# Two more quad products in the 512-column form, and a ScalarE copy ahead of a high part

## The reference

```python
D_FF = 2816
def swiglu(h, w_gate_up, w_down):
    gate, up = jnp.split(h @ w_gate_up, 2, axis=-1)
    return (jax.nn.silu(gate) * up) @ w_down
...
    h = h + swiglu(rms_norm(h, ffn_norm[layer]), ffn_w_gate_up[layer], ffn_w_down[layer])
```

## Time and profile before

| | before |
|---|---|
| median of 3 runs | 1299.03 us (1298.75 to 1299.54) |
| the profiled execution's own time | 1299.24 us |
| its span, first to last instruction | 1297.4 us |
| granted PE clock | 1.000, the upper level (2.4 GHz) |
| PE busy | 1285.9 us (99%), 7292 matmuls |
| DVE busy | 917.2 us (71%) |
| ACT busy | 556.1 us (43%) |

### The profile page before, as it was taken

One profiled execution on the slowest core, in us unless ns is written; L12 is line 12 of the kernel. 1 busy time (PEld: TensorE's weight loads), 2 busy tenths in 40 slices (PEclk: granted clock), 3 DMA queues, 4 the chain that ended last, 5 costly groups with the idle time before them and its releaser, 6 DMA issues.

```text
span 1297.4 us, 19358 instructions
## 1 busy us (share of the span) xinstructions
PE 1285.9 (99%) x7292; PEld 1102.0 (85%) x7292; DVE 917.2 (71%) x1413; ACT 556.1 (43%) x1162; POOL 255.7 (20%) x290
## 2 busy tenths in 40 slices
PE   9999999999999999999999999999999999999998
PEld 8888778888888998899988878888888998899986
DVE  7988857356689984388945778556789983488842
ACT  6347455124533660056622347425423650166612
POOL 0222144212322002100021136413221012000020
PEclk9999999999999999999999999999999999999999
DMA  7334322232333323333323331133333423333232
GB/s 248 102 94 113 93 78 84 82 97 89 123 98 98 114 82 101 97 114 110 99 85 113 109 115 56 51 97 97 98 97 98 122 90 98 100 112 99 82 98 98
DMA packets 96844, 130.69 MB, mean 101 GB/s; under 512 B 5329, under 2 KB 62161, under 8 KB 96753
## 3 DMA queue, kind: packets, MB, share of 16 engines
q1 hardware_dynamic: 94976, 127.29, 31.8%
q10 hardware_dynamic: 1776, 2.18, 0.6%
HBM read 124.67 MB, written 2.10 MB: 98 GB/s over the span
## 4 chain that ended last, share of the span: by engine, by line
PE 90%; DVE 5%; issue 2%; ACT 2%; DMA 0%; SPq 0%; DVEq 0%; ACTq 0%
PE ps L807 18%; PE ps L811 18%; PE ps L810 18%; PE ps L986 4%; PE ps L988 4%; PE ps L987 4%; PE ps L975 3%; PE ps L976 1%; PE ps L1469 1%; PE ps L1468 1%; PE ps L1465 1%; DVE ff_u L2180 1%; PE ps L1298 1%; PE ps L1314 1%; PE ps L1327 1%
## 5 line engine op out<-in xcount | busy, mean ns | idle before, releaser
L729 POOL TENSOR_SCALAR w_hi<-raw 128x1024 fp32r<-128x1024 f32 x156 | 182.7, 1172 | 941.0 <-PE ps L988 366.8
L1497 DVE TENSOR_TENSOR w_lo<-raw,w_hi 128x1024 fp32r<-128x1024 f32 x161 | 201.2, 1253 | 182.1 <-POOL w_hi L729 178.6
L807 PE MATMUL ps<-f_hi,w_hi 128*128 128x512 f32 x720 | 281.2, 391 | 0.2 <-DVEq L1893 0.2
L811 PE MATMUL ps<-f_hi,w_lo 128*128 128x512 f32 x720 | 280.2, 389 | 0.0
L810 PE MATMUL ps<-f_lo,w_hi 128*128 128x512 f32 x720 | 280.2, 389 | 0.0
L986 PE MATMUL ps<-z_both,quad_hi 128*128 128x256 f32 x640 | 182.2, 285 | 4.5 <-ACT copied L2744 4.5
L987 PE MATMUL ps<-z_both,quad_hi 128*128 128x256 f32 x640 | 181.1, 283 | 0.0
L807 PEld LDWEIGHTS ps<-f_hi,w_hi 128*128 128x128 f32 x720 | 135.1, 188 | 28.8 <-DVEq L1893 0.4
L811 PEld LDWEIGHTS ps<-f_hi,w_lo 128*128 128x128 f32 x720 | 135.1, 188 | 28.4
L810 PEld LDWEIGHTS ps<-f_lo,w_hi 128*128 128x128 f32 x720 | 135.2, 188 | 27.8
L986 PEld LDWEIGHTS ps<-z_both,quad_hi 128*128 128x128 f32 x640 | 121.5, 190 | 9.8 <-ACT copied L2744 6.9
(11 more groups left out here) (276 smaller groups left out, 2276.1 us busy)
## 6 DMA issues: line engine op xcount, KB each, us to landing
quad_raw<-in_w_gate_up SPq DMA_DIRECT2D x64, 512.0 KB
raw<-in_w_down SPq DMA_DIRECT2D x44, 512.0 KB
raw<-in_w_gate_up SPq DMA_DIRECT2D x48, 256.0 KB
raw<-in_w_out SPq DMA_DIRECT2D x20, 512.0 KB
raw<-in_w_in SPq DMA_DIRECT2D x19, 512.0 KB
raw<-in_xa_wkv SPq DMA_DIRECT2D x16, 512.0 KB
raw<-in_w_in SPq DMA_DIRECT2D x17, 256.0 KB
raw<-in_xa_wq SPq DMA_DIRECT2D x8, 512.0 KB
```

The lines of the kernel that those rows point to most:

```text
L729: pool.tensor_scalar(w_hi[:, slot], raw[:, slot], 1.0, 1.0, ALU.mult, ALU.mult).then_inc(s_hi, 1)
L807: ins = pe.matmul(o, whi, rhi, start=start, stop=False)
L811: return pe.matmul(o, wlo, rhi, start=False, stop=stop)
L1497: dve.tensor_tensor(w_lo[:, slot], raw[:, slot], w_hi[:, slot].bitcast(F32), ALU.subtract).then_inc(s_lo, 1)
```

## The change

Products 3 and 7 take the `quad_product_apart` form too, so four of the seven have it. The low and high data of such a product lie in neighbouring rows of one tile (`zq_r`) instead of far apart in `z_both`. Banks 2 and 3 of a quad now hold a low-data half as well: `copy_third_sum` copies a whole bank (512 columns, was 256), and DVE gets a new instruction per quad, `second_tile_apart`, which adds these halves to the second output tile. The silu, the multiply and the release of banks that waited for `second_tile` now wait for it. On ACT, `f_high(n - 1, 0)` moves from ahead of two weight high parts and `copy_second_sum` to just behind that copy.

```diff
@@ PE
-                        quad_product(l, q, 3, d, False)
+                        quad_product_apart(l, q, 3, d_wide, d)
                         pe.wait_ge(s_cp, COPIED[q, "u2"])
-                        quad_product(l, q, 7, a, False)
+                        quad_product_apart(l, q, 7, a_wide, a)
@@ DVE
+                    def second_tile_apart(n):
+
+                        ff = ff_u if n % 2 else ff_g
+                        dve.wait_ge(s_c, 3 * (QUAD0[l, c] + n) + 1)
+                        dve.tensor_tensor(halves(ff[:, 1, :]), halves(ff[:, 1, :]), bank_pair(qg, n, 2, 1),
+                                          ALU.add).then_inc(s_c, 1)
+
                     def gated(n, p):
 
                         q = QUAD0[l, c] + n
-                        dve.wait_ge(s_c, 2 * q + 2 - p)
+                        dve.wait_ge(s_c, 3 * q + 3 - p)
...
                         second_tile(n)
+                        second_tile_apart(n)
@@ ACT
-                        act.activation(home(qg, n, 3), home(qg, n, 1), ACT.Copy).then_inc(s_cp, 1)
+                        act.activation(ps[:, bank(qg + n, 3), :], ps[:, bank(qg + n, 1), :], ACT.Copy).then_inc(s_cp, 1)
...
                         weight_high(c, n, 4)
-                        if n and not up:
-                            f_high(n - 1, 0)
                         if more:
                             weight_high(c, n + 1, 5)
                             weight_high(c, n + 1, 2)
                         copy_second_sum(n)
+                        if n and not up:
+                            f_high(n - 1, 0)
...
                         copy_third_sum(n)
                         if not up:
-                            act.wait_ge(s_c, 2 * q + 1)
+                            act.wait_ge(s_c, 3 * q + 2)
                             act.activation(ff_g[:, 1, :], ff_g[:, 1, :], ACT.Silu).then_inc(s_q_silu, 1)
```

More of the change, by code:

```diff
@@ L70 @@
 Z_HIGHS = (1, 2, 4, 5, 6, 7, 3)
+APART = (2, 4, 3, 7)
+Z_STEP = {slot: 2 if slot in [Z_SLOT[i] for i in APART] else 1 for slot in range(8)}
+Z_UNIT = {slot: 4 * sum(Z_STEP[before] for before in range(slot)) for slot in range(8)}
+Z_HIGH_UNIT = {i: 4 * sum(Z_STEP.values()) + 4 * j for j, i in enumerate(i for i in Z_SLOT if i not in APART)}
 Z_LOWS = (1, 5, 2, 6, 3, 7, 4)
@@ L269, in trunk @@
         zf_hi, zf_lo = f_hi[:, 4:12, :], f_lo[:, 4:12, :]
[L270 to L274, removed]
+        zq = at("zq", [P, 60, QHALF], F32, z_zh)
+        zq_r = at("zq_r", [P, 60, QHALF], F32R, z_zh)
         quad_raw = at("quad_raw", [P, SLOTS, 4, 2 * P], F32, z_raw)
@@ L344, in low_and_high, with z_rows @@
         def low_and_high(i, k):
-            lo, hi = 4 * Z_SLOT[i] + k, 32 + 4 * (i - 1) + k
-            return z_both[:, lo:hi + 1:hi - lo, :]
+            u = Z_UNIT[Z_SLOT[i]] + 2 * k
+            return zq_r[:, u:u + 2, :]
+        def z_rows(i):
+            step = 2 if i in APART else 1
+            lo = Z_UNIT[Z_SLOT[i]]
+            hi = lo + 1 if i in APART else Z_HIGH_UNIT[i]
+            return slice(lo, lo + 3 * step + 1, step), slice(hi, hi + 3 * step + 1, step)
         def halves(tile):
@@ L975, in quad_product_apart @@
                     pe.matmul(both, kind_hi(i)[:, k, :], low_and_high(i, k), start=False, stop=False, skip_group_check=True)
-                    ins = pe.matmul(o, kind_lo(q, i)[:, k, :], zq_hi[:, i - 1, k, :], start=False, stop=k == 3,
+                    ins = pe.matmul(o, kind_lo(q, i)[:, k, :], low_and_high(i, k)[:, 1, :], start=False, stop=k == 3,
                                     skip_group_check=True)
@@ L984, in quad_product @@
                     whi, wlo = kind_hi(i)[:, k, :], kind_lo(q, i)[:, k, :]
-                    zh, zl = zq_hi[:, i - 1, k, :], zq_lo[:, Z_SLOT[i], k, :]
+                    lo, hi = z_rows(i)
+                    zh, zl = zq_r[:, hi, :][:, k, :], zq_r[:, lo, :][:, k, :]
                     pe.matmul(o, whi, zh, start=start and k == 0, stop=False, skip_group_check=True)
@@ L1003, in quads @@
                     b, a, d = home(g0, n, 0), home(g0, n, 1), home(g0, n, 2)
-                    b_wide, a_wide = ps[:, bank(g0 + n, 0), :], ps[:, bank(g0 + n, 1), :]
+                    b_wide, a_wide, d_wide = (ps[:, bank(g0 + n, i), :] for i in (0, 1, 2))
                     quad_product(l, q, 5, d, True)
@@ L2094, in z_scaled @@
                     for m in tiles:
-                        to = zq[:, 0:2, m, :] if m < 4 else zq[:, 2:4, m - 4, :]
+                        s0 = m // 4 * 2
+                        u0, u1 = (Z_UNIT[s] + Z_STEP[s] * (m % 4) for s in (s0, s0 + 1))
+                        to = zq[:, u0:u1 + 1:u1 - u0, :]
                         src = h[:, m, :].rearrange("p (a n) -> p a n", a=2)
@@ L2102, in wide @@
                     def wide(i):
-                        return zq[:, i].rearrange("p a n -> p (a n)")
+                        return zq[:, Z_UNIT[i]:Z_UNIT[i] + 3 * Z_STEP[i] + 1:Z_STEP[i], :]
                     dve.tensor_tensor(wide(to), wide(x), wide(y), op).then_inc(s_zs, 1)
@@ L2109, in z_low @@
                         dve.wait_ge(s_zqh, 7 * l + Z_HIGHS.index(i) + 1)
-                        dve.tensor_tensor(zq_lo[:, Z_SLOT[i]].rearrange("p a n -> p (a n)"),
-                                          zq[:, Z_SLOT[i]].rearrange("p a n -> p (a n)"),
-                                          zq_hi[:, i - 1].rearrange("p a n -> p (a n)").bitcast(F32),
+                        lo, hi = z_rows(i)
+                        dve.tensor_tensor(zq_r[:, lo, :], zq[:, lo, :], zq_r[:, hi, :].bitcast(F32),
                                           ALU.subtract).then_inc(s_zql, 1)
@@ L2156, in free @@
                     def free(n):
-                        dve.wait_ge(s_c, 2 * (QUAD0[l, c] + n) + 2)
+                        dve.wait_ge(s_c, 3 * (QUAD0[l, c] + n) + 3)
                         dve.nop().then_inc(s_free[(qg + n) % 2], 4)
@@ L2696, in z_high @@
                         act.wait_ge(s_zs, 12 * l + DB + {5: 1, 7: 2, 6: 3, 3: 4}[i])
-                    act.activation(zq_hi[:, i - 1].rearrange("p a n -> p (a n)"),
-                                   zq[:, Z_SLOT[i]].rearrange("p a n -> p (a n)"), ACT.Copy).then_inc(s_zqh, 1)
+                    lo, hi = z_rows(i)
+                    act.activation(zq_r[:, hi, :], zq[:, lo, :], ACT.Copy).then_inc(s_zqh, 1)
                 def weight_high(c, n, i):
@@ L2729, in copy_apart @@
                         if q:
-                            act.wait_ge(s_c, 2 * q)
+                            act.wait_ge(s_c, 3 * q)
                         act.activation(apart[:], bank_pair(qg, n, 0, 1), ACT.Copy).then_inc(s_apart, 1)
@@ L2737, in copy_fifth @@
                         if q:
-                            act.wait_ge(s_c, 2 * q - 1)
+                            act.wait_ge(s_c, 3 * q - 2)
                         act.activation(copied[:, 1, :], home(qg, n, 2), ACT.Copy).then_inc(s_cp, 1)
```

## The result

The changed kernel takes 1311.58 us in the median (1311.37 to 1311.81, 5 runs) against 1299.26 (1298.75 to 1299.54, 5 runs): ratio 1.0095, 95% interval 1.0082 to 1.0109. It is 12.3 us slower. The forecast was 1312.3.

A forecast was written before the change was run, and what follows sets the result against it. PE, busy 99% of the span, was taken as the bound, with DVE close behind. New waits of 22.6 us, minus 7.8 and 1.9, plus 0.4 for last quads, gave a median of 1312.3 us; range 1301 to 1319.

The forecast's parts named there:

- The pace of PE: On PE: a product of 12 narrow matmuls takes 1.44 us, a joined one 1.41.
- the sum: Whole kernel: 22.6 us of new waits, minus 7.8 and 1.9, is +12.9; last quads add 0.4; median 1312.3.
- The Trainium skill's rate: PE matmul issue: about 81 ns at 128 columns, 131 at 512; 256 joined steps would give back 17 us; not used.
- The ACT move: On ACT: u2 no longer stands behind f_high, which alone takes away twelve PE waits, 7.8 us.
- twelve waits: PE ahead of product 7 in even quads, waiting for the u2 copy: 0.65 us each, 7.8 in all.
- The cover that is gone: Ahead of product 3 in even quads: 0.65 us slack, 0.94 added by wider copy and new add, so PE waits.
- The walk: Two quads followed through PE, DVE and ACT: a turn takes 21.81 us, 20.69 before; 1306 to 1319, chance 0.72.
- PE's busy time: In the profile after: 7036 matmuls, 256 fewer, and less busy time in a longer span.
- The second rival: Only DVE's queue is late, ACT's catches up; even-quad waits ahead of 3 and 7 remain: +0.6, 1299.7 us; chance 0.14.
- The Trainium skill's rule on DVE: New add on DVE: (N + 151)/0.96, 691 ns at 512; as queue pace 22.1 us a turn, some 5 us later.

The follow-up runs named there:

- e3: Changed kernel without second_tile_apart and with the third sum's copy narrow again: 1291.97 us, ratio 0.9948.
- e1: Kernel before with only the ACT move of f_high behind copy_second_sum: 1292.80 us, ratio 0.9953.
- e4: Changed kernel with products 3 and 7 narrow again on PE, extra add and wide copy kept: 1312.70 us, ratio 1.0107.
- e10: Changed kernel with the gate tile's second silu on ACT behind the zeroing, c1 copy and apart copy: 1301.00 us, ratio 1.0017.
- e6: Kernel before with the ACT move and the odd quad's second f_low behind the next quad's low 6 on DVE: 1290.74 us, ratio 0.9936.

## Why the prediction was right

**The pace of PE** was read rightly. Joined products take 1.41 in turns without waits, narrow ones 1.44; e3 against e1 gives 0.8 us for the join, e4 against the changed kernel 1.5, of the 1.9 in the sum; by the lengths of the four runs of quads it is 0.5 and 0.8. At least a part of the remainder went into waits, as in e3's 7''. The Trainium skill's rate ("TensorE: Matmul & The Clock Gate", "Back-to-back issue gap"), by which the join would give back some 17 us, does not hold for these matmuls: a step over k takes 0.35 us in the joined form and 0.36 in the narrow one.

**The ACT move** was priced at 7.8 us, and measured 6.1 alone. This term was too large. The step took away twelve waits and put nothing in their place, while PE, no longer delayed, finds u2 late in the last quad of each run (0.17 us and a restart of 0.08, four times, 1.0 us). The four runs together gain 6.7 us; that the whole kernel gains 0.6 less is not explained by them.

**The cover that is gone** was the deciding step: 0.65 of slack, 0.94 put in front of it. The rows after show it used up: the low part of 3' ends at 582.65, 0.28 past the 582.37 at which 3' could have started.

**The walk** gave 21.81 a turn, and it is 21.63. The waits, without the restart, were forecast as 0.34, 0.32, 0.36 and 0.48, and are 0.43, 0.31, 0.29 and 0.24, with a fifth of 0.05 ahead of 3'' that the walk did not have. The first was too small, as the hand-over from DVE is longer (0.15 from 582.65 to 582.80, taken as 0.07). The last was too large, because u2 starts 0.19 earlier than in the walk. ACT starts the next instruction 0.48 after a PSUM copy of 512 columns (590.53 to 591.01), taken as 0.53, and 0.26 after one of 256 columns (590.27 to 590.53, 592.58 to 592.84), taken as about 0.3; PE also comes 0.06 later to 7''. A restart costs 0.07 behind the waits of the even quad (0.31 between the first two matmuls of a joined product, 0.24 otherwise) and 0.10 behind those of the odd quad (590.66 to 590.99 and the like), taken as 0.10 for each. The errors cancel in part, and that the total came within 0.7 us is in part luck.

By runs the sum came to +4.4 us for a run of ten and +2.2 for a run of six; measured are +4.0 and +2.3 to +2.4, 12.6 for the four together. The whole kernel is 12.3 longer; the difference of 0.3 arises outside the quads and is not explained. In a run of ten the three whole turns between 1' of the third quad and 1' of the ninth are 0.18 shorter than the walk, 0.5 together. In a run of six there is one such turn, and its first two quads take 18.8 to 18.9 us against 18.6 before: the rest of the plain tiles' work stands in DVE's queue there (two `f_lo` instructions behind the new add, 438.63 to 439.92), and PE waits 0.20 to 0.27 ahead of 7 of the first odd quad, which the walk had left out.

**PE's busy time** was forecast to fall, and rose by 7 us. The forecast took the matmuls' work for the busy time, and the profile counts short waits into it.

**The second rival** (DVE late alone, ACT catching up) has its kernel in e10: the two waits of the even quads and, twice, that of 7 in the first odd quad of a run of six, 1301.0, 1.9 above its before, for which the prediction had +0.6. It did not come about in the changed kernel, since the silu that waits for the new add stands ahead of c1.

**The Trainium skill's rule on DVE** ("VectorE: DVE Perf Modes", "The TRN2 errata") gives the duration of the new add, 691 ns against 687 measured. As a pace of the queue it would be too slow: independent instructions of this size start 0.60 apart (579.56 to 581.37 for three). The prediction's estimate of this rule's effect was also too high: 22.1 us a turn instead of 21.81 makes 3.5 us in twelve turns, not some 5.

## What to carry to other kernels

An engine that is busy for 86% of its stage can have no room at the head of a dependent chain, although the average says that it is idle for 14%: compare what is inserted ahead of a result with the slack of the first consumer that waits (0.65 against 0.94 here), not with idle time. When several queues wait for each other in a ring, walk one whole turn through all of them with start-to-start distances; single waits don't add up (the ACT move is worth 6.1 us in one kernel and under 1 in the other). And before giving up extra work as too dear, look for the instruction that makes an in-order queue stand: an `f_low` behind a round trip and a silu ahead of an urgent copy were the 19 us. Then compare both kernels in their mended order: here the one without the join (e6) came out ahead.

## What the runs showed of the hardware

A DVE or ACT instruction that needs nothing from the one before starts before that one's end: 0.60 against a duration of 0.69 on DVE at 512 columns, 0.53 against 0.62 on ACT, 0.48 after a 512-column copy out of PSUM. A dependent one pays the duration and 0.03 to 0.04. That difference decides whether 32 instructions fit into a 20 us turn (19.2 us) or not (22.1). A copy within PSUM costs what a copy from PSUM to SBUF does: 582 ns for 512 columns against 585.
